# State outputs of a hybrid S5 decoder layer over 128 stacked rows, by an exchange of halves through DRAM, and the table products in one piece

## The chip, the cores and the metric

One core of a Trainium2 chip runs the whole kernel. The metric is device time in microseconds, the median of several runs. All times below are microseconds, unless ns is said.

## What is computed

One decoder layer is run for a prompt of 512 tokens and for 8 samples of 8 tokens each, together T = 576 tokens of width 1024: input projection, attention, a state-space branch (S5), merge, MLP, and an embedding gate. The change lies in the S5 branch, whose essence is

```
bu_re = einsum('btgc,gpc->btgp', ug, bb_re)        # 32 groups g of 16 channels c, 64 states p
bu_im = einsum('btgc,gpc->btgp', ug, bb_im)
_, _, hr, hi = associative_scan(combine, (ar, ai, bu_re, bu_im), axis=1)
y = einsum('btgp,gcp->btgc', hr, c_re) - einsum('btgp,gcp->btgc', hi, c_im)
y = y.reshape(bsz, t, D_SSM) + d_skip * uf
```

## The kernel before, in words

The tokens are cut into 72 chunks of CH = 8. Within a chunk the S5 output is a product with a 128x128 table per group (`Tm`: 8 steps times 16 channels on either side). Across chunks only the state at the chunk's border counts: `Hb` holds it, as real and imaginary part, for 16 pairs of groups. On the 128 partitions lie the 64 states of the even group of a pair (rows 0 to 63) and of the odd group (rows 64 to 127). `CA` holds, in the same layout, the powers that take a border state to the 8 outputs of its chunk. The output of group g in a PSUM bank is `Tm[g] . UT[g]` (128 rows) plus two products of 64 rows, `CA re . Hb re` and `CA im . Hb im`.

Three kinds of TensorE work stand between the dense products in this stretch:
- table blocks (event `vs`): products `bb . CA`, 16 columns wide over 64 rows, of which `Tm` is made. ScalarE copies them from PSUM to the tile `vs`; GpSimd adds the skip term (event `vd`), stores `vs` to DRAM and, once it has landed (semaphore `vs_spilled`), reads it back into `Tm` in eight loads, one per 16 partitions (event `tload`, semaphore `t_in`).
- the scan over the chunk borders (events `scan` 0 to 5), on VectorE in `Hb`: two products, one sum over both parts, and two sums of one part each per level. Its own semaphore is `scanned`.
- output blocks 0 to 3 (event `y`): 8 groups each, into two banks; ScalarE applies gelu, GpSimd stores.

A dense unit is one 128-wide slice of the input weights against all 576 tokens: 48 matmuls (8 slices of the contraction, three products of high and low halves, two column ranges). It waits at its start for the low half of its weights (`w_lo`), which VectorE makes three units ahead, after ScalarE has cast the high half, and for its PSUM bank, of which there are two in turn. The units in question are, in order, the gate units G2, G3, G4, G5, G6, G7 and the value units V0, V1, V2, V3. ScalarE evicts a gate unit into `gst`, which has two slots; GpSimd stores each from there to DRAM. So the eviction of G7 waits until the store of G5 has landed (`gate_out`).

The order of the work is one list, written out in `schedule_of`. Each engine runs through it and does its part of every event, so the place of an event in the list is its place in every engine's queue: `event` adds it, `unit()` puts a dense unit there, `begin(4)` the first half of one. GpSimd's queue also holds the DMAs that it issues, SP's the weight loads.

In the order before, TensorE has: G2, table block of 32 matmuls, G3, block of 64, G4, block of 32, G5, G6, G7, V0, output block 0, half of V1, output 1, rest of V1, output 2, half of V2, output 3, rest of V2, the final states, V3.

Of the kernel before, what the change touches and what calls it, by code (L numbers as in the profile page):

```python
# [25 lines left out]
ALU = mybir.AluOpType  # L26
# [5 lines left out]
P = 128  # L32
# [92 lines left out]
def schedule_of(units):  # L125
# [214 lines left out]
    event("sfinal", place=0)  # L340
    unit()
# [222 lines left out]
def build(nc, i, o):  # L564
# [4 lines left out]
    with ctx:  # L569
# [277 lines left out]
        u_d = nc.dram_tensor("u_spill", [AT, CH, P, NCH], F32, kind="Internal").ap()  # L847
        y_d = nc.dram_tensor("y_spill", [CH, GC, G, NCH], F32, kind="Internal").ap()
# [97 lines left out]
        def full_of(job):  # L946
            return psum_full[jobs[job][0]]
# [8 lines left out]
        def read(job):  # L956

            return free_of(job), jobs[job][1] + 1
# [127 lines left out]
        def _(pool):  # L1086
# [85 lines left out]
            for e in schedule:  # L1172
# [25 lines left out]
                elif k == "vd":  # L1198
# [4 lines left out]
                    for n in (6, 7):  # L1203
                        pool.wait_ge(*read(("vs", n)))
# [15 lines left out]
                elif k == "tload":  # L1220
# [3 lines left out]
                    for n in range(CH):  # L1224
                        pool.dma_start(Tm[GC * n:GC * n + GC, :, GC * n:P],
                                      vs_d[:, :, 0:P - GC * n]).then_inc(t_in, 16)
                elif k == "y" and a[1] == 1:
# [97 lines left out]
        def _(scalar):  # L1325
# [137 lines left out]
            for e in schedule:  # L1463
# [107 lines left out]
                elif k == "vs":  # L1571
                    scalar.wait_ge(*full(e))
                    if a[0] == 0:
# [143 lines left out]
        def _(vector):  # L1717
# [147 lines left out]
            for e in schedule:  # L1865
# [220 lines left out]
                elif k == "final":  # L2086
# [3 lines left out]
                    for q in range(2):  # L2090
                        c = sq8[:, q, 0, :].unsqueeze(1).unsqueeze(3).to_broadcast([P, 2, GP, 9])
                        tt(t9[q][:], src, c, ALU.mult).then_inc(count.up(dve_steps), 1)
                    vector.wait_ge(*count.last)
# [196 lines left out]
        def _(tensor):  # L2290
# [205 lines left out]
            for e in schedule:  # L2496
# [85 lines left out]
                elif k == "vs" and a[0] % 2 == 0:  # L2582

                    both = [("vs", a[0] + odd) for odd in range(2)]
# [4 lines left out]
                    for c in range(4):  # L2589
                        for part in range(2):  # L2590
                            for odd in range(2):
                                g = 4 * a[0] + odd + 2 * c
                                r = slice(64 * odd, 64 * odd + 64)
                                ins = mm(bank(both[odd])[0:GC, P * c:P * c + P], bb[r, part, g // 2, :],
                                         CA[r, part, g // 2, 0:CH, :].rearrange("q k c -> q (k c)"), part == 0, part == 1)
                                if c == 3 and part == 1:
                                    ins.then_inc(full_of(both[odd]), 1)
# [37 lines left out]
                elif k == "y" and a[1] == 0:  # L2635
# [9 lines left out]
                    for c in range(4):  # L2645
                        out = [bank(job)[:, NCH * c:NCH * c + NCH] for job in both]
                        for odd in range(2):
                            g = 8 * q + 2 * c + odd
                            mm(out[odd], Tm[:, g, :], UT[:, g, :], True)
                        for part in range(2):  # L2650
                            for odd in range(2):
                                r = slice(64 * odd, 64 * odd + 64)
                                ins = mm(out[odd], CA[r, part, 4 * q + c, 1:CH + 1, :].rearrange("q k c -> q (k c)"),
                                         Hb[r, part, 4 * q + c, :], False, part == 1)
                                if c == 3 and part == 1:
                                    ins.then_inc(full_of(both[odd]), 1)
# [202 lines left out]
```

## Time and profile before

| | |
|---|---|
| median of 3 runs | 928.38 (928.04 to 929.18) |
| span of the profiled execution (its whole time is not given apart) | 926.8 |
| TensorE busy | 912.9, 98% |
| VectorE busy | 603.9, 65% |
| ScalarE busy | 442.2, 48% |
| GpSimd busy | 91.5, 10% |

In the timeline each row is a run of like instructions: start, busy time, engine, source line, operation, output and inputs, and how many. An f32 product is shown as two matmuls. A pair of brackets gives the idle time before the row and what ended it. The view of the transfers gives rates in 40 equal slices of its window and, for each issue, the time to landing.

### The profile page before, as it was taken

How to read it: one execution, taken by the hardware profiler on the slowest of the kernel's cores; microseconds unless marked ns; L12 is line 12 of the kernel's file. 1: busy time of each engine (PE TensorE's matmuls, PEld its weight loads, DVE VectorE, ACT ScalarE, POOL GpSimd, SP SyncE). 2: the span in 40 equal slices, each digit the busy share in tenths (PEclk: the TensorE clock that was granted, in tenths of full speed). 3: DMA queues.
4: the chain of work that ended last, by engine and by line, in shares of the span. 5: the costliest groups of instructions: out<-in, count | busy, mean ns of one | idle time of the engine just before them, and what ended most of it. 6: DMA issues, size and time to landing. Idle time of an engine off the chain costs nothing.

```text
span 926.8 us, 17665 instructions
## 1 busy us (share of the span) xinstructions
PE 912.9 (98%) x7414; PEld 886.4 (96%) x7414; DVE 603.9 (65%) x815; ACT 442.2 (48%) x663; POOL 91.5 (10%) x143
## 2 busy tenths in 40 slices
PE   6999999999999999999999999999999999999998
PEld 5999999999999889999999999999999999999998
DVE  6689699511777746474568566666676666778453
ACT  7446323223776535444356544444444444446532
POOL 5390033202001210100000000000000000000000
PEclk9999999999999999999999999999999999999999
DMA  8531554824423585522223322222323222242202
GB/s 234 127 92 48 151 160 109 185 84 147 128 71 108 186 286 204 172 69 71 89 69 92 91 86 83 87 89 91 92 79 91 84 90 92 91 138 71 69 5 99
DMA packets 134694, 102.19 MB, mean 110 GB/s; under 512 B 18560, under 2 KB 124408, under 8 KB 134584
## 3 DMA queue, kind: packets, MB, share of 16 engines
q1 hardware_dynamic: 129096, 83.38, 30.5%
q0 software_dynamic: 5424, 17.65, 6.2%
q8 instruction: 59, 0.97, 0.4%
q14 instruction: 19, 0.16, 0.1%
q10 hardware_dynamic: 96, 0.04, 0.0%
HBM read 88.71 MB, written 12.21 MB: 109 GB/s over the span
## 4 chain that ended last, share of the span: by engine, by line
PE 92%; DVE 3%; ACT 2%; issue 1%; DMA 0%; SPq 0%; ACTq 0%; DVEq 0%
PE dense L2294 65%; PE banks L2294 20%; PE scoreA L2294 3%; PE banks L2481 2%; PE dense L2481 1%; PE scoreB L2294 1%; DVE Llo L1745 1%; ACT t L1626 1%; DVE t L2118 1%; ACT whi L1333 1%; DMA xtok<-in_x_prompt 0%; DVE Ssum L1721 0%; DVE sm L2176 0%; DVE wlo L1745 0%; ACT yh L1672 0%
## 5 line engine op out<-in xcount | busy, mean ns | idle before, releaser
L1745 DVE TENSOR_TENSOR wlo<-wraw,whi 128x1024 fp32r<-128x1024 f32 (+2 forms) x139 | 152.6, 1103 | 101.3 <-ACT whi L1333 89.0
L2294 PE MATMUL dense<-hid,whi 128*128 128x256 f32 (+1 forms) x1024 | 176.7, 294 | 0.1
L2294 PE MATMUL dense<-act_hi,whi 128*128 128x256 f32 (+1 forms) x736 | 167.4, 298 | 1.0 <-issue 0.7
L2294 PE MATMUL dense<-act_lo,whi 128*128 128x256 f32 (+1 forms) x736 | 163.3, 293 | 0.0
L2294 PE MATMUL dense<-act_hi,wlo 128*128 128x256 f32 (+1 forms) x736 | 163.3, 293 | 0.0
L2294 PEld LDWEIGHTS dense<-hid,whi 128*128 128x128 f32 x1024 | 152.5, 187 | 0.5 <-issue 0.3
L1333 ACT CAST whi<-wraw 128x1024 fp32r<-128x1024 f32 x100 | 109.9, 1101 | 45.6 <-PE banks L2294 44.1
L2294 PEld LDWEIGHTS dense<-act_hi,whi 128*128 128x128 f32 x736 | 123.4, 188 | 4.7 <-issue 3.3
L2294 PEld LDWEIGHTS dense<-act_lo,whi 128*128 128x128 f32 x736 | 124.1, 188 | 0.0
L2294 PEld LDWEIGHTS dense<-act_hi,wlo 128*128 128x128 f32 x736 | 124.0, 187 | 0.0
L2294 PE MATMUL dense<-hid,wlo 128*128 128x256 f32 (+1 forms) x512 | 108.8, 293 | 0.0
L2294 PEld LDWEIGHTS dense<-hid,wlo 128*128 128x128 f32 x512 | 85.4, 187 | 0.0
L2294 PE MATMUL banks<-XT,whi 128*128 128x288 f32 x416 | 83.7, 294 | 0.0
L1349 ACT CAST whi<-wsum 128x512 fp32r<-128x512 f32 x52 | 32.3, 621 | 86.3 <-PE dense L2294 63.6
L1826 DVE TENSOR_TENSOR R<-R,dense 128x576 f32<-128x576 f32 x64 | 48.0, 750 | 34.9 <-PE dense L2294 34.9
L2294 PEld LDWEIGHTS banks<-XT,whi 128*128 128x128 f32 x416 | 66.4, 188 | 0.0
L2294 PE MATMUL banks<-XT,wlo 128*128 128x288 f32 x208 | 61.3, 295 | 0.0
L2294 PE MATMUL dense<-yh,whi 128*128 128x256 f32 (+1 forms) x256 | 47.9, 300 | 0.5 <-ACT sg L1424 0.3
L1144 POOL DMA_DIRECT2D ptok<-in_p_prompt x4 | 2.2, 550 | 445.2 <-PE banks L2294 433.2
L2294 PE MATMUL banks<-act_hi,wlo 128*128 128x288 f32 x156 | 45.9, 294 | 0.0
L2294 PE MATMUL banks<-act_lo,whi 128*128 128x288 f32 x156 | 45.9, 294 | 0.0
L2294 PE MATMUL banks<-act_hi,whi 128*128 128x288 f32 x156 | 45.8, 294 | 0.0
(367 smaller groups left out, 1590.4 us busy)
## 6 DMA issues: line engine op xcount, KB each, us to landing
wraw<-in_w_in SPq DMA_DIRECT2D x32, 512.0 KB, 5.1
wraw<-in_w_up SPq DMA_DIRECT2D x32, 512.0 KB, 4.0
wraw<-in_w_down SPq DMA_DIRECT2D x32, 512.0 KB, 3.6
gates_spill<-gst POOLq DMA_DIRECT2D x16, 288.0 KB, 3.0
page<-in_cache_k SPq DMA_DIRECT2D x16, 256.0 KB, 7.9
page<-in_cache_v SPq DMA_DIRECT2D x16, 256.0 KB, 7.3
wraw<-in_w_out SPq DMA_DIRECT2D x8, 512.0 KB, 3.7
wraw<-in_w_ple_gate SPq DMA_DIRECT2D x8, 512.0 KB, 3.6
```

The lines of the kernel that those rows point to most:

```text
L1144: pool.dma_start(ptok[0:n, t % 2, :], src).then_inc(x2_in[t % 2], 16)
L1333: nc.scalar.copy(by_channel(u, whi[:, wslot(u), :]), by_group(u, wraw[:, u % NRAW, :])).then_inc(count.up(w_hi), 1)
L1349: nc.scalar.copy(wblock(whi, u, j), src).then_inc(count.up(w_hi), 1)
L1626: nc.scalar.activation(t1[h % 2][:], zflat(h), ACT.Exp, bias=bias[:, h:h + 1]).then_inc(count.up(z_free), 1)
L1745: return nc.vector.tensor_tensor(out=lo, in0=whole, in1=f32(hi), op=ALU.subtract)
L1826: nc.vector.tensor_tensor(out=R[:, m % 8, :], in0=R[:, m % 8, :], in1=prod(job), op=ALU.add).then_inc(count.upto(*read(job)), 1)
L2118: nc.vector.scalar_tensor_tensor(out=t2[h % 2][:], in0=zflat(h), scalar=bias[:, h:h + 1], in1=t1[h % 2][:], op0=ALU.add, op1=ALU.max).then ...
L2294: return nc.tensor.matmul(out, lhsT, rhs, start=start, stop=stop, skip_group_check=True)
L2481: return nc.tensor.transpose(out, in_, ident[0:rows, 0:rows])
```

## The change

1. The table products are one event pair in place of four, directly after G2. The four pairs of groups of a quarter go to four column groups (output partitions 0, 32, 64, 96), the two groups of a pair to two banks. ScalarE copies the result in eight copies of the same size as before.
2. After the Tm loads, GpSimd exchanges halves of `CA` through DRAM: the imaginary part of rows 0 to 63 and the real part of rows 64 to 127 go out, and each comes back in the other's place. Afterwards part 0 holds real and imaginary part of the even group in 128 rows, part 1 those of the odd group. The same is done with `Hb` behind the scan.
3. The output blocks use one product of 128 rows per group for the states. They stand one and a half dense units later: V0, V1, half of V2, output 0, rest of V2, output 1, half of V3, output 2, rest of V3, output 3.
4. The final states are formed right behind the last scan level; the exchange waits for them (`scanned` 7).

```diff
@@ schedule_of
     for lvl in range(6):
         event("scan", lvl)
+        if lvl == 5:
+            event("final")
         unit()
...
-        for i in ((), (0, 1), (2, 3, 4, 5), (6, 7), (), ())[lvl]:
-            event("vs", i, place=2 * (i // 2 % 2) + i % 2)
+        if lvl == 1:
+            for odd in range(2):
+                event("vs", odd, place=odd)
         if lvl == 3:
             event("vd")
             event("tload")
+            event("swap_out", "tables")
+            event("swap_in", "tables")
         if lvl in (3, 4):
             unit()
+    event("swap_out", "states")
+    event("swap_in", "states")
+    unit()
+    begin(4)
     for q in range(4):
         for side in range(2):
             event("y", q, side, place=2 * (q % 2) + side)
         if q % 2 == 0:
+            unit()
+        else:
             begin(4)
-        else:
-            unit()
-        if q == 0:
-            event("final")
...
     event("sfinal", place=0)
     unit()
-    unit()
@@ GpSimd
+                elif k in ("swap_out", "swap_in"):
...
+                    if k == "swap_out":
...
+                            pool.wait_ge(scanned, 7)
+                        pool.dma_start(memory[0], part_im[0:NS]).then_inc(vs_spilled, 16)
+                        pool.dma_start(memory[1], part_re[NS:P]).then_inc(vs_spilled, 16)
+                    else:
+                        pool.wait_ge(vs_spilled, 16 * (3 if a[0] == "tables" else 5))
+                        pool.dma_start(part_re[NS:P], memory[0]).then_inc(t_in, 16)
+                        pool.dma_start(part_im[0:NS], memory[1]).then_inc(t_in, 16)
@@ ScalarE
-                    g0 = 8 * (a[0] // 2)
-                    nc.scalar.copy(vs[:, g0 + a[0] % 2:g0 + 8:2, :],
-                                   bank(e)[0:GC, :].rearrange("p (a b) -> p a b", a=4)).then_inc(
-                                       count.upto(*read(e)), 1)
+                    for c in range(4):
+                        ins = nc.scalar.copy(vs[:, 2 * c + odd:G:8, :],
+                                             bank(e)[32 * c:32 * c + GC, :].rearrange("p (a b) -> p a b", a=4))
+                    ins.then_inc(count.upto(*read(e)), 1)
@@ TensorE, vs
-                    for c in range(4):
+                    for n in range(4):
                         for part in range(2):
-                            for odd in range(2):
-                                g = 4 * a[0] + odd + 2 * c
-                                r = slice(64 * odd, 64 * odd + 64)
-                                ins = mm(bank(both[odd])[0:GC, P * c:P * c + P], bb[r, part, g // 2, :],
-                                         CA[r, part, g // 2, 0:CH, :].rearrange("q k c -> q (k c)"), part == 0, part == 1)
...
+                            for c in range(4):
+                                for odd in range(2):
+                                    r = slice(64 * odd, 64 * odd + 64)
+                                    ins = mm(bank(both[odd])[32 * c:32 * c + GC, P * n:P * n + P], bb[r, part, 4 * n + c, :],
+                                             CA[r, part, 4 * n + c, 0:CH, :].rearrange("q k c -> q (k c)"),
+                                             part == 0, part == 1)
@@ TensorE, y
-                        tensor.wait_ge(t_in, 16 * CH)
-                        tensor.wait_ge(scanned, 6)
+                        tensor.wait_ge(t_in, 16 * (CH + 4))
...
                         for odd in range(2):
                             g = 8 * q + 2 * c + odd
-                            mm(out[odd], Tm[:, g, :], UT[:, g, :], True)
-                        for part in range(2):
-                            for odd in range(2):
-                                r = slice(64 * odd, 64 * odd + 64)
-                                ins = mm(out[odd], CA[r, part, 4 * q + c, 1:CH + 1, :].rearrange("q k c -> q (k c)"),
-                                         Hb[r, part, 4 * q + c, :], False, part == 1)
...
+                            mm(out, Tm[:, g, :], UT[:, g, :], True)
+                            ins = mm(out, CA[:, odd, 4 * q + c, 1:CH + 1, :].rearrange("q k c -> q (k c)"),
+                                     Hb[:, odd, 4 * q + c, :], False, True)
```

GpSimd's queue from the skip term on, before (`psum_free5` and `psum_free4` are the evictions of the dense bank that the gate to be stored was in):

```order
L1095 TENSOR_TENSOR dti<-ident,dd 16x512
L1095 TENSOR_TENSOR vs<-vs,dti 16x32x16 [waits psum_free3,psum_free2,pool_steps]
L1207 DMA vs_spill<-vs 16x4096 [waits vs_ready]
L1225 DMA Tm<-vs_spill 16x4096 [waits vs_spilled,tm_zero]
...
L1225 DMA Tm<-vs_spill 16x32x16
L1248 DMA gates_spill<-gst 128x576 [waits psum_free5]
L1248 DMA gates_spill<-gst 128x576 [waits psum_free4]
L1248 DMA gates_spill<-gst 128x576 [waits psum_free5]
L1231 DMA y_spill<-ygelu 128x576 [waits psum_free1,psum_free0]
```

and with the change, from the last Tm load on:

```order
L1233 DMA Tm<-vs_spill 16x32x16
L1247 DMA ca_spill<-CA 64x2304 [waits psum_full1,psum_full0]
L1248 DMA ca_spill<-CA 64x2304
L1251 DMA CA<-ca_spill 64x2304 [waits vs_spilled]
L1252 DMA CA<-ca_spill 64x2304
L1274 DMA gates_spill<-gst 128x576 [waits psum_free5]
L1274 DMA gates_spill<-gst 128x576 [waits psum_free4]
L1274 DMA gates_spill<-gst 128x576 [waits psum_free5]
L1247 DMA hb_spill<-Hb 64x1152 [waits scanned]
L1248 DMA hb_spill<-Hb 64x1152
L1251 DMA Hb<-hb_spill 64x1152 [waits vs_spilled]
L1252 DMA Hb<-hb_spill 64x1152
```

The four table transfers, with a wait between them, stand ahead of the gate stores of G5, G6 and G7, and the four of the states behind them.

TensorE at output block 0, before:

```order
L2294 MATMUL banks<-UT,Tm 128x72 [waits psum_free0,psum_free1,scanned,t_in]
L2294 MATMUL banks<-UT,Tm 128x72
L2294 MATMUL banks<-Hb,CA 128x72 x4
L2294 MATMUL banks<-UT,Tm 128x72 x2
L2294 MATMUL banks<-Hb,CA 128x72 x4
```

and with the change:

```order
L2322 MATMUL banks<-UT,Tm 128x72 [waits psum_free1,psum_free0,t_in]
L2322 MATMUL banks<-Hb,CA 128x72
L2322 MATMUL banks<-UT,Tm 128x72
L2322 MATMUL banks<-Hb,CA 128x72
L2322 MATMUL banks<-UT,Tm 128x72
```

The block has 16 f32 products instead of 24, and 72 more dense matmuls stand ahead of the first.

## Rows read from the trace of the kernel before

**Rows 1.** The page: busy times of the engines, share of the span, instructions

```profile
PE 912.9 (98%) x7414; PEld 886.4 (96%) x7414; DVE 603.9 (65%) x815; ACT 442.2 (48%) x663; POOL 91.5 (10%) x143
```

**Rows 2.** Timeline, TensorE: the table blocks, and the start of G6

```profile
130.67 0.43 PE L2294 MATMUL dense<-act_hi,wlo 128*128 128x256 f32 x2
131.03 1.92 PE L2294 MATMUL banks<-CA,bb 64*16 64x128 f32 x32
132.89 0.53 PE L2294 MATMUL dense<-act_hi,whi 128*128 128x256 f32 x2
...
139.41 3.67 PE L2294 MATMUL banks<-CA,bb 64*16 64x128 f32 x64
...
157.81 0.43 PE L2294 MATMUL dense<-act_hi,whi 128*128 128x256 f32 x2
158.07 0.42 PE L2294 MATMUL dense<-act_lo,whi 128*128 128x256 f32 x2
```

**Rows 3.** Timeline, TensorE: output block 0 and what follows it

```profile
176.77 0.56 PE L2294 MATMUL banks<-UT,Tm 128*128 128x72 f32 x4
177.26 0.67 PE L2294 MATMUL banks<-Hb,CA 64*128 64x72 f32 x8
...
181.44 0.53 PE L2294 MATMUL dense<-act_hi,whi 128*128 128x256 f32 x2
181.81 0.42 PE L2294 MATMUL dense<-act_lo,whi 128*128 128x256 f32 x2
```

**Rows 4.** Timeline, VectorE: scan level 3 and the low halves around it

```profile
145.39 1.22 DVE L1745 TENSOR_TENSOR wlo<-wraw,whi 128x1024 fp32r<-128x1024 f32 x1
146.64 3.89 DVE L1721 TENSOR_TENSOR sc<-Hb,sq 128x1760 f32<-128x1760 f32 x2
150.57 5.93 DVE L1721 TENSOR_TENSOR Hb<-Hb,sc 128x1760 f32<-128x1760 f32 x3
156.42 2.35 DVE L1745 TENSOR_TENSOR wlo<-wraw,whi 128x1024 fp32r<-128x1024 f32 x2
```

**Rows 5.** Timeline, GpSimd (POOL): from G4's gate store to G7's

```profile
150.58 0.54 POOL L1248 DMA_DIRECT2D gates_spill<-gst  x1 [9.57 <-ACT gst L1414]
155.85 0.56 POOL L1207 DMA_DIRECT2D vs_spill<-vs  x1 [0.29 <-POOL vs L1095]
160.62 4.91 POOL L1225 DMA_DIRECT2D Tm<-vs_spill  x8 [4.21 <-DMA vs_spill<-vs]
165.53 1.13 POOL L1248 DMA_DIRECT2D gates_spill<-gst  x2
175.37 0.54 POOL L1248 DMA_DIRECT2D gates_spill<-gst  x1 [8.71 <-ACT gst L1414]
```

**Rows 6.** Timeline, ScalarE: the eviction of G7

```profile
174.42 0.65 ACT L1414 ACTIVATE gst<-dense 128x576 f32<-128x576 f32 x1 [8.50 <-DMA gates_spill<-gst]
```

**Rows 7.** Timeline, TensorE: 20 transposes; 16 matmuls on four column groups

```profile
122.51 2.35 PE L2481 MATMUL banks<-ident,qk 128*128 128x128 f32 x20
...
341.61 0.65 PE L2294 MATMUL scoreA<-KTb,Qb 128*32 128x128 f32 x16
```

**Rows 8.** Transfers issued from 140 to 210: KB each, median us to landing

```profile
wraw<-in_w_in SPq DMA_DIRECT2D x8, 512.0 KB, 4.2
y_spill<-ygelu POOLq DMA_DIRECT2D x4, 288.0 KB, 2.4
vs_spill<-vs POOLq DMA_DIRECT2D x1, 256.0 KB, 4.2
...
Tm<-vs_spill POOLq DMA_DIRECT2D x1, 32.0 KB, 8.1
```

**Rows 9.** Transfers, 380 to 388: 40 slices, the last eight x_sample's (64 partitions)

```profile
GB/s 164 184 246 225 348 389 348 471 348 430 471 369 430 410 369 348 451 394 435 438 300 382 438 415 404 369 379 394 422 430 351 179 166 184 159 156 146 236 156 207
```

**Rows 10.** Timeline, TensorE: the first transposes of 128x128

```profile
8.54 3.67 PE L2481 MATMUL dense<-ident,xtok 128*128 128x128 f32 x16 [0.60 <-DVE xtok L1874]
12.05 2.20 PE L2481 MATMUL banks<-ident,xtok 128*128 128x128 f32 x15
```

More of the change, by code:

```diff
@@ L1202, in _ @@
                     pool.wait_ge(*count.last)
-                    for n in (6, 7):
-                        pool.wait_ge(*read(("vs", n)))
+                    for odd in range(2):
+                        pool.wait_ge(*read(("vs", odd)))
                     tt(vs[:, :, 0:GC], vs[:, :, 0:GC], dti[:], ALU.add).then_inc(count.up(vs_ready), 1)
@@ L1226, in _ @@
                                       vs_d[:, :, 0:P - GC * n]).then_inc(t_in, 16)
+                elif k in ("swap_out", "swap_in"):
+                    part_re, part_im, memory = (
+                        (CA[:, 0].rearrange("p g k c -> p (g k c)"), CA[:, 1].rearrange("p g k c -> p (g k c)"), ca_d)
+                        if a[0] == "tables" else
+                        (Hb[:, 0].rearrange("p g n -> p (g n)"), Hb[:, 1].rearrange("p g n -> p (g n)"), hb_d))
+                    if k == "swap_out":
+                        if a[0] == "tables":
+                            for odd in range(2):
+                                pool.wait_ge(*full(("vs", odd)))
+                        else:
+                            pool.wait_ge(scanned, 7)
+                        pool.dma_start(memory[0], part_im[0:NS]).then_inc(vs_spilled, 16)
+                        pool.dma_start(memory[1], part_re[NS:P]).then_inc(vs_spilled, 16)
+                    else:
+                        pool.wait_ge(vs_spilled, 16 * (3 if a[0] == "tables" else 5))
+                        pool.dma_start(part_re[NS:P], memory[0]).then_inc(t_in, 16)
+                        pool.dma_start(part_im[0:NS], memory[1]).then_inc(t_in, 16)
                 elif k == "y" and a[1] == 1:
@@ L2091, in _ @@
                         c = sq8[:, q, 0, :].unsqueeze(1).unsqueeze(3).to_broadcast([P, 2, GP, 9])
-                        tt(t9[q][:], src, c, ALU.mult).then_inc(count.up(dve_steps), 1)
-                    vector.wait_ge(*count.last)
+                        tt(t9[q][:], src, c, ALU.mult).then_inc(count.up(dve_steps if q == 0 else scanned), 1)
+                    vector.wait_ge(dve_steps, count.made[dve_steps])
+                    vector.wait_ge(scanned, 7)
                     tt(Fh[:], Fh[:], t9[0][:], ALU.add).then_inc(count.up(dve_steps), 1)
@@ L2581, in _ @@
                     ins.then_inc(full_of(e), 1)
-                elif k == "vs" and a[0] % 2 == 0:
-                    both = [("vs", a[0] + odd) for odd in range(2)]
+                elif k == "vs" and a[0] == 0:
+                    both = [("vs", odd) for odd in range(2)]
                     tensor.wait_ge(ca_ready, 1)
@@ L2588, in _ @@
                             tensor.wait_ge(*free(job))
-                    for c in range(4):
+                    for n in range(4):
                         for part in range(2):
-                            for odd in range(2):
-                                g = 4 * a[0] + odd + 2 * c
-                                r = slice(64 * odd, 64 * odd + 64)
-                                ins = mm(bank(both[odd])[0:GC, P * c:P * c + P], bb[r, part, g // 2, :],
-                                         CA[r, part, g // 2, 0:CH, :].rearrange("q k c -> q (k c)"), part == 0, part == 1)
-                                if c == 3 and part == 1:
-                                    ins.then_inc(full_of(both[odd]), 1)
+                            for c in range(4):
+                                for odd in range(2):
+                                    r = slice(64 * odd, 64 * odd + 64)
+                                    ins = mm(bank(both[odd])[32 * c:32 * c + GC, P * n:P * n + P], bb[r, part, 4 * n + c, :],
+                                             CA[r, part, 4 * n + c, 0:CH, :].rearrange("q k c -> q (k c)"),
+                                             part == 0, part == 1)
+                                    if n == 3 and part == 1 and c == 3:
+                                        ins.then_inc(full_of(both[odd]), 1)
                 elif k in ("kout", "vout"):
@@ L2645, in _ @@
                     for c in range(4):
-                        out = [bank(job)[:, NCH * c:NCH * c + NCH] for job in both]
                         for odd in range(2):
                             g = 8 * q + 2 * c + odd
-                            mm(out[odd], Tm[:, g, :], UT[:, g, :], True)
-                        for part in range(2):
-                            for odd in range(2):
-                                r = slice(64 * odd, 64 * odd + 64)
-                                ins = mm(out[odd], CA[r, part, 4 * q + c, 1:CH + 1, :].rearrange("q k c -> q (k c)"),
-                                         Hb[r, part, 4 * q + c, :], False, part == 1)
-                                if c == 3 and part == 1:
-                                    ins.then_inc(full_of(both[odd]), 1)
+                            out = bank(both[odd])[:, NCH * c:NCH * c + NCH]
+                            mm(out, Tm[:, g, :], UT[:, g, :], True)
+                            ins = mm(out, CA[:, odd, 4 * q + c, 1:CH + 1, :].rearrange("q k c -> q (k c)"),
+                                     Hb[:, odd, 4 * q + c, :], False, True)
+                            if c == 3:
+                                ins.then_inc(full_of(both[odd]), 1)
                 elif k == "zz":
```

5 lines of the change are left out of this document (4 added, 1 removed).

## The prediction

> **What bounds the kernel now.** I read the page first, then TensorE in order of time around the two places that the change touches, then VectorE, ScalarE and GpSimd over the same stretch, and last the transfers. TensorE is busy 98% of the span [rows 1]: what counts is work on TensorE, or time for which it is made to wait. In this stretch it is never idle: a dense unit of 48 matmuls is 24 pairs that start 0.26 us apart (157.81 to 158.07 [rows 2]), 6.33 us in all.
>
> The table blocks stand between G2 and G5 with 32, 64 and again 32 matmuls [rows 2] (an f32 product is two matmuls in the trace). The first holds up the dense stream from 130.67 + 0.26 = 130.93 to 132.89, and the first dense pair after it takes 0.37 instead of 0.26 (181.44 to 181.81 [rows 3]): 2.06 us. The second, by its 3.67 instead of 1.92 us, costs 3.8, the third 2.06 again: together 7.9. The four output blocks cost 4.67 + 0.11 = 4.78 us each: in one, four runs of 4 table matmuls and four of 8 state matmuls alternate, (181.44 - 177.26) / 7 = 0.60 us a run behind the first [rows 3], although the 8 state matmuls run two by two (upper and lower 64 rows at once) and fill only four places.
>
> VectorE is the hidden second bound. From 145 to 169 its instructions follow one another with no idle time [rows 4]: scan level 3, then the low halves of G6's and G7's weights, the first ready at 156.42 + 1.21 = 157.63. G6 starts at 157.81 [rows 2]. So G6 has 0.2 us to spare, no more.
>
> GpSimd's queue is the third. It stores G4's gate at 150.58, the vs table at 155.85, waits 4.2 us for it, issues the eight Tm loads from 160.62, and only then stores G5's and G6's gates (165.53) [rows 5]. ScalarE therefore evicts G7 only at 174.42, after 8.50 us of waiting for G5's store [rows 6]. That costs nothing today because V1, which reuses G7's PSUM bank, starts after output block 0, at 181.44 [rows 3].
>
> **The change on TensorE.** Output blocks: 32 matmuls of full 128 rows, no switch between 64 and 128 rows. 20 transposes with weights of the same 128x128 take 2.35 us, the last one's tail of 0.27 included [rows 7], 0.11 each. At 0.112 a place a block takes 32 x 0.112 = 3.6 us against 4.78. Saved: 4 x 1.2 = 4.9 us. The number of places is unchanged; only the switches go.
>
> Table block: 128 matmuls, now 8 at once (four groups of 16 columns times two halves of rows). Four at once, on four column groups, are in the trace: 16 matmuls in 0.65 us, the last one's tail of 0.27 included [rows 7], so 0.1 for four. With 8 at once: 16 places x 0.11 + 0.3 = 2.1 us, saved 5.8; bounds 2.1 and 7.3 (only the halves overlap, as now).
>
> **Where the table saving goes.** The first block keeps its length, so G3 still ends at 139.3. G4 then follows at once and ends at 145.6, 3.8 us earlier. G5 waits for its low half (145.39 + 1.22 = 146.6) and ends at 152.95. G6 waits for 157.63, for the scans are where they were: TensorE idles 4.7 us. Of 5.8 us, 0.1 is left at G6's start. What is late next is VectorE. G7 ends at 170.4, V0 at 176.7, as before.
>
> ScalarE's eight copies (as many as before and of the same size, two after each old small block) now stand in one run of some 4 us from 133.0, ahead of a cast whose low half VectorE takes up at 145.39 [rows 4]: no cost, as long as those 7 us of slack stand.
>
> **Where the exchanges go.** They are GpSimd's, in its queue ahead of G5's gate store, and the second half of each waits for the first to land. All 3.8 us earlier than before: G4's store 146.8, first Tm load 156.8. Before, the last Tm load landed at 164.9 + 8.1 = 173.0 [rows 5, 8], 12.4 us after the first issue; now 169.2. Then:
> - tables out: two transfers of 576 KB from 64 partitions. The one plain 64-partition transfer, the x_sample load, moves 146 to 184 GB/s where the 128-partition ones before it move 350 to 450 [rows 9]. 590 kB / 0.19 = 3.1 us each, 6.2: landed 175.4.
> - GpSimd resumes 0.55 us after a landing (155.85 + 4.2, next issue 160.62 [rows 5, 8]). A single y_spill of 288 KB lands in 2.4 us [rows 8], 0.8 of it data at 380 GB/s, so 1.6 us is fixed. Tables in: 176.0 + 1.6 + 6.2 = 183.8.
> - G5's store lands 0.8 us later, 184.6; half a microsecond for weight loads between: **ScalarE evicts G7 at about 185.0** (174.42 before).
>
> V1 now comes straight after V0 and needs that bank: TensorE can go at 176.7 and is let go at 185.7. Stall 9.0 us.
>
> Unknown is whether two transfers on opposite halves overlap. If they did fully, both would move at 380 and each leg would take 3.1. The eight Tm loads go to eight different groups of 16 partitions, and 1152 KB of them need 12.4 us; the one vs store from 16 partitions moves 256 KB in 4.2 [rows 8]. They did not overlap, so I take them one after the other. The Trainium skill, in "SBUF — State Buffer", section "Can I just issue two DMAs to hit both halves?", speaks against this exchange: two transfers at partitions 0 and 64 gave 6% more than one. By that page, as an estimate, the eviction comes at 184.3.
>
> State exchange: issued behind G7's store, which starts 0.95 us after the eviction (175.37 against 174.42 [rows 5, 6]). Out: 1.6 + 0.8 (G7's data) + 2 x 1.55 = landed 6.4 after the eviction; back: 0.55 + 1.6 + 3.1: 11.7 after it. TensorE gets to block 0 at 0.7 + 9.5 (V1 and half of V2) = 10.2 after it, so it would wait 1.5 us. But after 9 us of standing still I expect the clock to have fallen from 2.4 to 1.2 GHz: in the old trace the granted clock reads 1.00 (2.4 GHz) in every slice, yet the first 16 transposes after the idle start take 3.67 us, and the next 15 take 2.20 with two of them still slow [rows 10]. Some 20 matmuls at 0.1 more each: 1.8 us, which makes it 12.0 and covers the state exchange. Block 0 starts at 197.0 either way within 0.3.
>
> The Trainium skill ("DMA: Bandwidth & Descriptors", "Anatomy of one DMA — SWDGE (gpsimd) path") has a fixed 2.0 us for such a transfer where rows 8 give 1.6. By it, as an estimate, three legs take 0.4 us more each and the sum is about 1 us higher.
>
> **Sum.** Before, block 0 starts at 176.77 with 72 dense matmuls (9.5 us) fewer behind it: comparable 186.3. Now 197.0: +10.7. Output blocks -4.9. Everything after is the same work and follows TensorE. +5.8 us on a span of 926.8. The profiled execution's span is 1.6 us under the median; on the median of 928.4 that is **934.2 us**. About 0.2% (1.9 us) is what a measurement can tell from no change.
>
> **Rivals.**
> - A, the halves overlap or run at full rate (13%). Two legs of 3.1 us less: eviction at 178.8, stall 2.8 us, no fall of the clock, block 0 at 189.0: 2.7 - 4.9 = -2.2, 926.2 us. For it: 128-partition transfers reach 380 GB/s. Against it: [rows 8, 9]. This is the side of faster, and it decides at an eviction near 181.1: the exchanges have to be 4 us shorter than my sum.
> - B, weight loads of SP take the engines between (10%). Eight loads of 512 KB lie in 70 us of the old trace, each 1.4 us of all engines at 380 GB/s [rows 8], and they come in pairs after the paired casts. If a pair lies in front of the tables and one load in front of the states: +3 and +1.5, 938.7 us. For it: the load of 512 KB lands in 4.2 us at the median, so it is itself held up by what lies in front.
> - C, the 8 groups don't run at once (8%). Block of 7.3 us: G4 ends 1.5 later than before instead of 3.8 earlier, and the whole GpSimd chain with it: +5.2, 939.4 us. Four at once only: +1.7.
> - D, the saving arrives whole (4%): neither the gate stores nor the scans hold TensorE, 928.4 - 4.9 - 5.8 = 917.7. Against it stands VectorE without a gap [rows 4]. If only the gate store doesn't hold it: 928.4 - 5.0 = 923.4.
>
> **Numbers.** My forecast has 65%: 929 to 937 on its own, by 4 us less in the table legs or 3 more. Below 0.2% slower lie A, D and a tenth of the forecast's own share. Faster 0.13 (most of A, and D), same 0.11 (rest of A, short end of the forecast), slower 0.76. Range 926.5 to 939.0: both ends of the transfer rate but one in five left out (D, the worst of B and C).
>
> **What would show it.** Right: one table block of about 2 us at 131.0; TensorE idle before G6 by 4 to 5 us, released by VectorE; the four table transfers on GpSimd between 161.7 and 177, a gap of 10 us or more between out and in; ScalarE's G7 eviction at 183 to 187 and TensorE idle from 176.7 until just after; output blocks of 3.6 us without a switch. Wrong: an eviction before 181; a table block over 4 us; G6 starting well before 157.6; output blocks still near 4.7.

## The result, and the profile after

The changed kernel takes **937.66** in the median of six executions (936.89 to 943.19), against 928.67 for the kernel before, measured beside it: a ratio of 1.0114, 95% interval 1.0099 to 1.0128, so between 9 and 12 us slower. Four executions lie between 936.9 and 937.7, two at 942.2 and 943.2. The forecast had 934.2. The profiled execution took 937.27, with a span of 935.5, 8.7 over that of before [rows 1]. Its first table block starts 0.41 later than that of before, so 0.41 has to be taken off times from here on when they are set beside the old ones.

From its page, busy times and the granted clock in 40 slices:

```profile
PE 906.8 (97%) x7350; PEld 882.5 (94%) x7350; DVE 604.4 (65%) x815; ACT 443.1 (47%) x663; POOL 96.3 (10%) x151
...
PEclk9999998989999999999999999999999999999999
```

TensorE is busy for 6.1 us less, though the span is longer: it is made to wait. The two slices that read 8 (140 to 164 and 187 to 210) hold the stretches at a low clock behind the two long waits. The timeline of TensorE, with the table block, the two long waits and the start of output block 0:

```profile
131.44 2.00 PE L2322 MATMUL banks<-CA,bb 64*16 64x128 f32 x128
...
158.12 0.85 PE L2322 MATMUL dense<-act_hi,whi 128*128 128x256 f32 x2 [4.53 <-DVE wlo L1772]
...
188.44 0.82 PE L2322 MATMUL dense<-act_hi,whi 128*128 128x256 f32 x2 [9.14 <-ACT gst L1440]
...
200.88 0.44 PE L2322 MATMUL banks<-UT,Tm 128*128 128x72 f32 x2 [0.58 <-DMA Hb<-hb_spill]
201.16 0.39 PE L2322 MATMUL banks<-Hb,CA 128*128 128x72 f32 x2
201.38 0.39 PE L2322 MATMUL banks<-UT,Tm 128*128 128x72 f32 x2
```

The block of 128 matmuls, 2.00 us long, stands in place of three that were busy for 1.92, 3.67 and 1.92 [rows 2]. G6 still starts where it did, behind 4.53 us of idling until VectorE has its low half. V1 starts at 188.44, after 9.14 us for ScalarE's eviction of G7. Output block 0 starts at 200.88 instead of 176.77 [rows 3] with 9.5 us of dense work moved ahead of it, so 14.6 late (14.2 with the 0.41 taken off). Inside the block a pair of matmuls starts every 0.22 us, without the pattern of fours and eights.

ScalarE's eviction of G7 and, on GpSimd, the transfers ahead of it:

```profile
187.64 0.65 ACT L1440 ACTIVATE gst<-dense 128x576 f32<-128x576 f32 x1 [19.37 <-DMA gates_spill<-gst]
```

```profile
157.93 4.91 POOL L1233 DMA_DIRECT2D Tm<-vs_spill  x8 [4.09 <-DMA vs_spill<-vs]
162.84 0.58 POOL L1247 DMA_DIRECT2D ca_spill<-CA  x1
...
178.00 0.53 POOL L1251 DMA_DIRECT2D CA<-ca_spill  x1 [14.06 <-DMA ca_spill<-CA]
...
179.03 1.13 POOL L1274 DMA_DIRECT2D gates_spill<-gst  x2
```

The stores of G5's and G6's gates are issued at 179.03 (165.53 before [rows 5]), because GpSimd stands for 14.06 us between the two halves of the table exchange. ScalarE stands behind that for 19.37 us, where it was 8.50 before [rows 6]. The transfers issued between 140 and 215, KB each and median us to landing:

```profile
wraw<-in_w_in SPq DMA_DIRECT2D x9, 512.0 KB, 6.4
...
ca_spill<-CA POOLq DMA_DIRECT2D x2, 576.0 KB, 13.8
CA<-ca_spill POOLq DMA_DIRECT2D x2, 576.0 KB, 7.8
...
Tm<-vs_spill POOLq DMA_DIRECT2D x1, 32.0 KB, 12.0
```

The last Tm load takes 12.0 us to land instead of 8.1 [rows 8], so all are in at 162.3 + 12.0 = 174.3, 16.4 after the first issue instead of 12.4. The weight loads of SP take 6.4 instead of 4.2. The two kinds share the engines, which the windows show (us, TensorE busy, granted clock, DMA share, GB/s):

```profile
160.00:164.00 4.00, 4.00 (x24) 0.70 1.06 174
164.00:172.00 8.00, 8.00 (x63) 1.00 1.12 137
172.00:177.00 5.00, 5.00 (x40) 1.00 1.03 334
177.00:180.00 3.00, 2.29 (x18) 1.00 1.22 293
180.00:186.00 6.00, 0.00 (x0) 0.74 0.99 240
```

By the DMA share all 16 engines are busy from 160 to 186, at very different rates; the rates are those of all queues together. And the same view around the two long waits:

```profile
153.00:158.00 5.00, 0.59 (x5) 0.76 0.46 52
156.00:158.00 2.00, 0.00 (x0) 0.50 0.00 0
158.00:162.00 4.00, 3.88 (x16) 0.50 0.80 102
162.00:166.00 4.00, 4.00 (x31) 0.95 1.18 191
...
183.00:188.00 5.00, 0.00 (x0) 0.50 0.66 190
188.00:192.00 4.00, 3.56 (x15) 0.50 0.61 146
192.00:194.00 2.00, 2.00 (x13) 0.71 0.82 235
194.00:200.00 6.00, 6.00 (x48) 1.00 0.92 247
```

Behind both waits TensorE works at a granted clock of 0.50 (1.2 GHz): 16 and 15 matmuls in 3.9 and 3.6 us of work, where a window of 4 us at full clock holds up to 33. The clock has fallen before the waits end: at 155.6, 2.0 us into the first, and at 182.9, 3.6 us into the second. It is back at 162.4 and at 193.1. So it is low for 6.8 and for 10.2 us, and TensorE has work in 4.3 and 4.7 us of that. The forecast had this behind the second wait only.

### The profile page after: what moved, and what is told of

It reads as the page before. It is cut to its first block, busy times and chain, and to the rows that moved or that the text cites. A ratio compares the mean times of both kernels' runs of the same rounds, so it can differ in the third digit from the quotient of the medians.

```text
span 935.5 us, 17543 instructions
## 1 busy us (share of the span) xinstructions
PE 906.8 (97%) x7350; PEld 882.5 (94%) x7350; DVE 604.4 (65%) x815; ACT 443.1 (47%) x663; POOL 96.3 (10%) x151
## 4 chain that ended last, share of the span: by engine, by line
PE 86%; DMA 5%; DVE 3%; ACT 3%; POOL 1%; issue 1%; SPq 0%; ACTq 0%; DVEq 0%; POOLq 0%
PE dense L2322 60%; PE banks L2322 19%; PE scoreA L2322 3%; PE banks L2509 2%; DMA ca_spill<-CA 2%; DMA gates_spill<-gst 1%; PE scoreB L2322 1%; DMA xtok<-in_x_prompt 1%; DVE Llo L1772 1%; DMA Hb<-hb_spill 1%; ACT t L1653 1%; DVE t L2146 1%; ACT whi L1359 1%; DMA hb_spill<-Hb 1%; POOL Tm L1233 0%
## 5 line engine op out<-in xcount | busy, mean ns | idle before, releaser
L2322 PEld LDWEIGHTS dense<-act_hi,whi 128*128 128x128 f32 x736 | 125.1, 190 | 18.9 <-issue 12.1
```

The costliest lines, as they stand in the source:

```text
L2322: return nc.tensor.matmul(out, lhsT, rhs, start=start, stop=stop, skip_group_check=True)
```

## Experiments

All times are medians; the kernel before, beside them, had 928.2 to 928.6. Granted clocks and waits are those of the one profiled execution of each.

**Where the table exchange stands.** In this kernel it comes directly behind the table products; the numbers of `vs_spilled` that are waited for change with it.

```diff
         if lvl == 1:
             for odd in range(2):
                 event("vs", odd, place=odd)
+            event("swap_out", "tables")
+            event("swap_in", "tables")
         if lvl == 3:
             event("vd")
             event("tload")
-            event("swap_out", "tables")
-            event("swap_in", "tables")
```

> The changed kernel, with the exchange of the tables issued by GpSimd directly behind the table products (before G3's gate store) instead of behind the eight Tm loads; its counts of landed transfers are renumbered to suit, nothing else. Theory (the stall comes from the place of the table exchange in GpSimd's queue): the tables are out and back by 150, G5's store lands near 174, ScalarE evicts G7 at 174 to 175, V1 starts by 177.5, the state exchange (some 12 us) lies wholly beside V1 and half of V2 or ends 1 to 2 us behind them, output block 0 starts near 187 to 189; 923.5 to 926 us. Rival (SP's weight loads that share the DMA engines, not the place in the queue, make the delay): Tm's last load still lands 16 us after the first is issued, G7's eviction comes at 177 to 178, V1 waits 1 to 2 us and the state exchange 3 more: 928 to 930 us.

Measured: 924.94 (five executions, four of them 924.8 to 925.2, one 932.2, its mean clock 0.993 where the others have 0.996 to 0.998), span 923.2. Because of the one, the ratio's interval holds 1: 0.9951 to 1.0015. GpSimd and ScalarE in its timeline:

```profile
133.70 0.55 POOL L1247 DMA_DIRECT2D ca_spill<-CA  x1 [0.99 <-PE banks L2322]
...
141.78 0.51 POOL L1251 DMA_DIRECT2D CA<-ca_spill  x1 [6.99 <-DMA ca_spill<-CA]
...
162.47 0.58 POOL L1274 DMA_DIRECT2D gates_spill<-gst  x1
```

```profile
173.79 0.65 ACT L1440 ACTIVATE gst<-dense 128x576 f32<-128x576 f32 x1 [5.50 <-DMA gates_spill<-gst]
```

The exchange is the same, the weight loads too; it now lies beside G3 and G4. G7 is evicted at 173.79 instead of 187.64, V1 has no wait, and block 0 starts at 188.62 without one. The medians differ by 12.7 us, and 12.1 of it is in the trace of the change: 9.14 of waiting ahead of V1, 2.4 of low clock behind it, 0.58 at block 0. The rival of the expectation, the weight loads, is not enough by itself to hold V1: the last Tm load still takes 11.3 us to land here, and nobody waits for it.

**No exchange at all**, and **no exchange with the old output products**. The first leaves out the eight transfers, so that its output blocks multiply unexchanged halves, and what TensorE waits for ahead of block 0 changes with it; the second puts back the old products as well.

```diff
-            event("swap_out", "tables")
-            event("swap_in", "tables")
...
-    event("swap_out", "states")
-    event("swap_in", "states")
```

> The changed kernel without both exchanges (eight transfers left out); the output blocks keep their new products of 128 rows, so the S5 outputs are computed from unexchanged halves. Theory: no stall ahead of V1, no fall of the clock there; the new order costs nothing by itself, the table products give nothing, and the four output blocks save 4.9 us together: 923.5 us (923 to 924.5). Rival (the later place of the output blocks or the longer waiting of the scan chain costs by itself): 926 us or more.

> The changed kernel without both exchanges and with the old output products (one of 128 rows, two of 64 rows per group), in the new order. Theory (the switches between products of 128 and of 64 rows cost 1.2 us per output block): 4.9 us above the run without the exchanges, so level with the kernel before, 928.4 us (within 0.7). Rival (most of the gain of the new blocks is in places, or hidden): less than 2.5 us above the run without the exchanges.

Measured: 924.80 (ratio 0.9964, 0.9950 to 0.9978) and 930.42 (1.0020, 1.0010 to 1.0030). Without the exchange the kernel is no faster than with the early one: moved, the exchange is hidden wholly. The starts of output blocks 0 and 1 in the two timelines, new products first:

```profile
188.82 0.34 PE L2318 MATMUL banks<-UT,Tm 128*128 128x72 f32 x2
...
195.56 0.34 PE L2318 MATMUL banks<-UT,Tm 128*128 128x72 f32 x2
```

```profile
189.26 0.56 PE L2318 MATMUL banks<-UT,Tm 128*128 128x72 f32 x4
...
197.19 0.56 PE L2318 MATMUL banks<-UT,Tm 128*128 128x72 f32 x4
```

6.74 against 7.93 from one block to the next, with the same dense work between: 1.19 a block, 4.8 in all, as the prediction worked out (1.2 and 4.9). The medians differ by more, 5.6; the other 0.8 was not traced. And the two kernels are 1.3 and 2.0 us slower than was expected. Both traces have a wait of 4.4 to 4.5 us ahead of G6 and a granted clock of 0.50 behind it; the next kernel shows what that costs.

**The table products alone**, in the kernel before.

```diff
-        for i in ((), (0, 1), (2, 3, 4, 5), (6, 7), (), ())[lvl]:
-            event("vs", i, place=2 * (i // 2 % 2) + i % 2)
+        if lvl == 1:
+            for odd in range(2):
+                event("vs", odd, place=odd)
```

> The kernel before with only the table products changed: one event pair of 128 matmuls behind G2, eight copies. Theory (VectorE's scan 3 and the low half of G6's weights hold G6 at 157.8, so the 5.8 us saved are given back as a wait ahead of G6): TensorE idle 4 to 5 us before G6, time within 0.5 us of the kernel before; if the clock falls after that wait, up to 2 us slower. Rival (the saving arrives whole): 922.6 us.

Measured: 930.51 (1.0024, 1.0015 to 1.0034): **2.1 us slower**, although 5.8 us of work are gone. The windows around G6:

```profile
153.00:158.00 5.00, 0.57 (x5) 0.99 0.46 52
158.00:162.00 4.00, 4.00 (x19) 0.58 0.84 108
162.00:166.00 4.00, 4.00 (x33) 1.00 1.18 195
```

TensorE waits 4.43 us for VectorE and then runs 19 matmuls in 4 us. Granted 0.58 of full speed for 4 us, it loses 1.7 us, and nothing behind it takes that up. The other executions lose as much or more: six of the ten have a mean clock of 0.995 or 0.996, the profiled one 0.998. So the saving doesn't merely vanish in the wait: the clock falls behind the wait, and the kernel gets slower.

**The same with that wait removed**: VectorE makes the low half of G6's weights ahead of scan level 3.

```diff
-        event("scan", lvl)
+        if lvl != 3:
+            event("scan", lvl)
         unit()
+        if lvl == 3:
+            event("scan", lvl)
```

> The kernel before with the new table products alone and scan level 3 behind its dense unit. The new products alone were 2.1 us slower than the kernel before, with TensorE idle for 4.4 us ahead of G6 and the granted clock at 0.50 behind it. Theory: with that wait gone the clock stays at 1.00 and part of the 5.8 us saved arrives: V0 starts 3 us earlier, output block 0 then waits for the scans (final level at 174.4) or for Tm (173 to 174.5), 926 us (925 to 927.5), that is 3.5 to 5 us under the run of the products alone. Rival: the clock falls all the same, 928.4 us or more.

Measured: 924.68 (0.9958, 0.9941 to 0.9974), 5.8 under the products alone. The clock stays at 1.00, and one wait of 1.29 is left, ahead of V0:

```profile
153.00:158.00 5.00, 5.00 (x40) 1.00 0.61 80
158.00:162.00 4.00, 4.00 (x33) 1.00 0.90 119
```

That is more than the 3.5 to 5 expected.

**The same step in the kernel with the early exchange.**

> The kernel with the tables exchanged early, and scan level 3 put behind the dense unit whose event it stood ahead of, so that VectorE makes the low half of G6's weights before it. Theory (the wait of 4.5 us ahead of G6 costs itself and 2.1 us more, since the granted clock is 0.50 for some 3.5 us behind it): no wait ahead of G6, granted clock 1.00 throughout, at most 2 us of wait ahead of V0 instead, block 0 at 186 to 187 because the state exchange (10.4 us from the last scan at 176) now holds it: 2 to 2.5 us under the run with the tables exchanged early, 922.5 us (921.5 to 923.5). Rival (the granted clock falls for another reason, such as the table products themselves): the slow stretch stays, 924.5 us or more.

Measured: 928.88 (1.0010, 1.0000 to 1.0019), so **4 us slower** than without the step; the expectation (922.5) missed. Start of output block 0, and windows:

```profile
187.53 0.44 PE L2325 MATMUL banks<-UT,Tm 128*128 128x72 f32 x2 [3.98 <-DMA Hb<-hb_spill]
```

```profile
183.00:187.00 4.00, 0.55 (x5) 1.00 0.92 220
188.00:198.00 10.00, 10.00 (x47) 0.50 0.08 30
198.00:204.00 6.00, 6.00 (x51) 0.98 0.00 0
```

Up to block 0 it went nearly as expected: no wait ahead of G6, block 0 at 187.5 (186 to 187 expected), 1.1 earlier than without the step, the state exchange now in the way. What was not expected is behind it: after 3.98 us of idling at a granted clock of 1.00 the clock is 0.50 for 10.2 us (188.0 to 198.2), all of it with work on TensorE, and 5.1 us go. The forecast's idea that a wait costs its length, and some 2 us if it is a long one, was too simple. The clock was low just as long around the 9.14 us wait of the changed kernel, but 5.5 of those 10.2 us lay in the wait itself. What sets the length of the low stretch, 3.4 to 10.2 us in these traces, was not tested.

**Weight loads held back**, to take them away from the Tm loads and the tables in the changed kernel:

```diff
+                if u == FIRST["v"] + 3:
+                    sync.wait_ge(t_in, 16 * CH)
+                elif u == FIRST["v"] + 4:
+                    sync.wait_ge(t_in, 16 * (CH + 2))
                 weights(u)
```

> The changed kernel; SP holds back the weight loads of V3 and of the three units behind it: the first two until the eight Tm loads have landed, the next until the tables are back. Theory (the weight loads share the DMA engines with the Tm loads at 160 to 168 and with the tables' way back at 177 to 180, and that is why ScalarE's eviction of G7 came 2.2 us later than forecast): the last Tm load lands 12.5 to 13 us after the first issue instead of 16.4, the tables out follow at once, G7's eviction comes 3 to 5 us earlier, at 183 to 184.5; 933 to 935 us. Rival (the Tm loads are slow in themselves, and the engines have room for both): landing and eviction within 1 us of the changed kernel's, 937 us; if the weights then come too late for their casts, slower still.

Measured: 940.31 (1.0133, 1.0116 to 1.0150). GpSimd and ScalarE:

```profile
157.58 4.90 POOL L1237 DMA_DIRECT2D Tm<-vs_spill  x8 [4.11 <-DMA vs_spill<-vs]
...
172.40 0.53 POOL L1255 DMA_DIRECT2D CA<-ca_spill  x1 [8.82 <-DMA ca_spill<-CA]
```

```profile
182.99 0.65 ACT L1444 ACTIVATE gst<-dense 128x576 f32<-128x576 f32 x1 [15.05 <-DMA gates_spill<-gst]
```

The mechanism held: the wait between the two halves is 8.8 instead of 14.1, the last Tm load lands 8.0 after its issue instead of 12.0, and G7 is evicted at 182.99 instead of 187.64 (4.3 earlier, since the times of this trace run 0.35 ahead of those of the change). The time did not (933 to 935 expected): the delayed loads fall on the state exchange, and the wait moves to output block 0 (3.16 us), with the same price as above:

```profile
195.00:199.00 4.00, 1.05 (x8) 1.00 0.93 211
199.00:209.00 10.00, 9.79 (x46) 0.53 0.12 41
```

**Output blocks half a unit later in the changed kernel**, for the two executions at 942 to 943.

> The changed kernel with the output blocks half a dense unit later, nothing else. In the changed kernel's profiled execution block 0 waited 0.6 us for the state exchange and the clock held, yet two of its six executions took 5 us longer. Theory (in those two the wait at block 0 was longer and the clock fell behind it, as in the run with a wait of 4.0 us there): with some 3 us of slack ahead of block 0 no execution is 5 us longer, all lie within 1.5 us of 937.0. Rival (they come from elsewhere): one execution in three is again 4 to 6 us above the others.

Measured: 937.88 (four executions, 936.98 to 938.45; 1.0101, 1.0086 to 1.0115). In line with the theory (no wait at block 0 in its trace, but one of 0.91 us ahead of the transposes of V); but if two executions in six are long ones, four in a row without one come by chance one time in five. The two long executions of the changed kernel were not profiled. Their mean granted clock was 0.987, that of the other four 0.990 to 0.993, so more time at the low clock is on record; that a wait at block 0 brought it is likely, not shown.

**Towards the best order.** The kernel with the early exchange and scan 3 behind its unit, its output blocks one unit later; then with the products of the final states (`sfinal`) ahead of output block 3 as well; then that with the blocks only half a unit later:

```diff
     unit()
-    begin(4)
+    unit()
     for q in range(4):
+        if q == 3:
+            event("sfinal", place=0)
         for side in range(2):
             event("y", q, side, place=2 * (q % 2) + side)
         if q % 2 == 0:
-            unit()
-        else:
             begin(4)
+        else:
+            unit()
...
-    event("sfinal", place=0)
-    unit()
```

> The kernel with the tables exchanged early and scan level 3 behind its unit, and now the output blocks one dense unit later (V0, V1, V2, half of V3, output 0, ...). The same without this step took 928.9 us with output block 0 ready at 187.5 after 4.0 us of waiting for the state exchange and the granted clock at 0.50 for the 10 us behind it. Theory (the wait costs its 4.0 us and 5 us of clock): TensorE reaches block 0 near 190, without waiting, the clock stays at 1.00 all the way: 919.5 us (918.5 to 921). Rival (the output blocks are slow for another reason, or their later place costs elsewhere, such as the later gelu and the y stores): 924 us or more.

> As the run with the output blocks one dense unit later (923.5 us; 921.7 to 927.5, TensorE waited 0.8 us for the copy of the final states and 0.95 for those of the values, directly behind the last output block), with the final states' products moved ahead of output block 3. Theory (those 1.8 us and some of the spread come from the final states standing between the last block and the values): both waits go, 921.5 us (920.5 to 922.5), spread under 2 us. Rival (the values' copies on ScalarE are behind the last gelu in any case): one wait of 1 to 2 us stays, 923 us or more.

> Tables exchanged early, scan level 3 behind its unit, output blocks half a unit later, and the final states' products ahead of output block 3. The state exchange ended at 187.5 in the run without the last two steps, TensorE reaches block 0 at 186.7: a wait of 0.8 us or less. Theory (it is the length of the wait that decides on the clock: 0.8 to 1.3 us left it at 1.00 elsewhere, 3.2 and 4.0 us did not): no fall of the clock in most executions, 920.5 us (919.5 to 922), perhaps single ones 5 us longer. Rival: any wait ahead of the output blocks brings the clock down, 926 us or more.

Measured, in this order: 923.46 (0.9956, 0.9939 to 0.9972; seven executions from 921.65 to 927.49), 923.88 (0.9952, 0.9939 to 0.9965) and **920.85** (0.9926, 0.9913 to 0.9940). One unit later, the wait at block 0 and the fall of the clock are gone, but the time is 4 us above the 919.5 expected: now the transposes of V behind the last block wait (0.8 us for the copy of the final states, 0.95 for that of the values; the other 2 were not traced, and the mean clock of the slower executions, down to 0.996, has a part in the spread). With `sfinal` ahead of block 3 they wait 2.38 us for the copy of the values alone, and ScalarE, which makes it, waits for the y store:

```profile
217.37 2.51 ACT L1598 COPY vtok<-banks 128x512 f32<-128x512 f32 x5 [3.04 <-DMA y_spill<-ygelu]
```

So that expectation missed, and its rival held. With half a unit between block 3 and the values that wait is gone too. Block 0 is reached 0.17 us before the states arrive (timeline), and the clock holds (window):

```profile
187.18 0.44 PE L2325 MATMUL banks<-UT,Tm 128*128 128x72 f32 x2 [0.17 <-DMA Hb<-hb_spill]
```

```profile
180.00:190.00 10.00, 9.83 (x79) 1.00 0.76 199
```

920.85 beats the kernel before by 7.8 us and the change by 16.8; five of its six executions lie between 920.7 and 921.2, one is at 924.8, with a mean granted clock of 0.996 where the others have 0.999 or 1.00. There is no slack at block 0: TensorE already waits 0.17 us there.

## Why the prediction was right and wrong

The direction and the chain were right: slower, by a table exchange that stands ahead of the gate stores in GpSimd's queue and so holds ScalarE's eviction of G7 and with it V1. The size was not: +5.8 forecast, +8.7 in the profiled execution, +9 in the median, and more in the mean. The step that failed is the transfer sum up to the eviction of G7, in its term for weight loads (0.5 us there, 4.3 by the run with the loads held back); second to it, the clock behind the wait of G6 and the price of the one behind V1's. By the steps of the prediction:

- *Output blocks, -4.9.* Right: -4.8, from the distance of the blocks.
- *Table block, 2.1 us, and its saving gone.* Right as to the block (2.00) and the wait (4.53 against 4.7). **Wrong that this is all**: the clock falls behind it. In the change its 2.1 us are covered, since V1 waits for GpSimd and not for TensorE. With the products alone they were the whole result. The step weighed a fall of the clock for the 9 us wait and left it out for the 4.7 us wait, with nothing in the trace to part the two.
- *"Half a microsecond for weight loads between".* **This term was mis-sized**, and it is the larger miss: the eviction came 2.2 us later (187.64 - 0.41 against 185.0). The last Tm load landed 4.7 later than forecast (174.3 - 0.4 against 169.2): 4.0 by the longer loads, 0.7 because GpSimd's work on the skip term took that much longer (147.83 to 152.99 against 151.13 to 155.56), so that they began 3.1 us earlier than before and not 3.8. Holding the weight loads back removed 4.3 us. The eviction then came at 182.9 in the old trace's time, 1.6 ahead of the forecast without its half microsecond: the loads cost 4.3 instead of 0.5, and the transfers themselves were forecast 1.6 too long, which hid part of the miss. The prediction had the mechanism as rival B with one part in ten. It should have been in the sum: the first Tm load is issued together with two weight loads (157.93 and, in SP's queue, 158.10) which in the old trace were issued ahead of it (from 157.66 on, against 160.62), and the tables meet the next ones (167.35 and 169.56, some 13 us to landing). The Trainium skill ("DMA: Bandwidth & Descriptors", "Queues, rings and completion order") says that each engine serves the queues with work in turn, packet by packet. The traces agree as far as they can show it: loads of both queues take half as long again here, and the Tm loads go back to 8.0 us with the other queue held back.
- *The two halves one after the other at 190 GB/s, behind the Tm loads.* Too slow for the way out. By the view of the transfers, the bytes (MB) of GpSimd's queue (q0) and SP's (q1), in the change from 174.3, where the last Tm load has landed, to 177.5, and in the kernel with the early exchange from 135.5 to 139:

```profile
q1 hardware_dynamic: 1101, 0.55, 58.4%
q0 software_dynamic: 91, 0.60, 45.5%
...
q0 software_dynamic: 111, 0.84, 105.1%
q1 hardware_dynamic: 5, 0.00, 0.2%
```

Only 0.60 of the tables' 1.18 MB moved behind the last Tm load. The rest had gone beside the Tm loads: from 163.4 to 174.3 GpSimd's queue moved 1.48 MB, more than all eight Tm loads together (1.18). So the tables were out 3.1 us behind it and not 6.2. The rate of GpSimd's queue was 188 GB/s beside 172 of SP's, and 240 with hardly anything of SP's. The 334 of the window 172 to 177 are both queues and the end of the Tm loads. On the way back (180 to 186) all queues together moved 240, G5's and G6's stores among it, and the leg took 9.6 us up to the eviction instead of 9.0. The 190 were read from slices [rows 9] in which SP's queue has a part (0.17 of the 0.39 MB from 386 to 388), and two of the eight slices read 236 and 207. The Trainium skill ("SBUF — State Buffer", section "Can I just issue two DMAs to hit both halves?") gives 6% for the second half; as an estimate from that page's figure on the 190, the pair would move 201. The 240 are above that, but the 190 themselves come from mixed slices, and no run here has one half alone, so the 6% can be neither confirmed nor refuted.
- *A stall of 9.0 ahead of V1.* 9.14, and that is luck: the eviction came 2.2 later than forecast, and TensorE got there 2.2 later too (178.9 in the old trace's time against 176.7), held up by the low clock behind G6's wait.
- *From V1 to block 0, 11.3.* 12.4: the clock cost 2.4 (0.50 for the 4.7 us up to 193.1) instead of 1.8, and block 0 waited 0.58 for the states, which were said to be covered within 0.3.
- *Everything after follows TensorE.* Not quite: TensorE is 9.9 us late at 234.8 and 9.15 late at 387.1, and the span ends 8.7 late. Shortly ahead of 387 the old trace has 0.35 us of idling on TensorE that this one lacks; what took up the rest was not traced.

So block 0 starts at 200.47 in the old trace's time instead of 197.0: 2.3 from the transfers (with the restart behind the eviction), 1.1 from clock and wait. That is the miss in the profiled execution. Two executions in six lie 5 us above the rest. The amount is that of a low clock behind a wait at block 0, as in two kernels here, but those executions were not traced. The range stopped at 939.0 since no case had it.

## What to carry to other kernels

Where transfers move ahead of others in one queue, ask first whether they can stand where nobody waits behind them: the same exchange cost 12.7 us behind the Tm loads and nothing behind the products that last read the tables. A wait put onto TensorE has two prices, its length and what the low clock takes from the work behind it, 1.7 to 5.1 us in these traces; a saving that only turns into a wait of 4 us can make the kernel slower. And when a chain of transfers is moved by a few microseconds, look at which loads of other queues it now meets, and put them into the sum, not into a rival.

## What the runs showed of the hardware that was not expected

- Around waits of 4.4 to 9.1 us ahead of a dense unit the granted clock fell to 0.50, and the length of the wait did not say what it cost: 1.7 us behind the 4.43 us wait of the products alone (low from 157.9 to 161.4, all behind the wait), 2.1 behind the 4.53 us wait of the change (155.6 to 162.4), 2.8 behind the 4.83 us wait ahead of V1 with the loads held back (182.5 to 189.4), 2.4 behind the wait of 9.14 us (182.9 to 193.1). Lost is half of the part in which TensorE had work.
- Waits of 3.2 and 4.0 us ahead of an output block (32 matmuls 72 wide) were followed by 10.2 us at 0.50, without idle time on TensorE: 5 us lost, more than the wait itself. What came behind these waits differs from the cases above, and so does where in the low stretch the wait ended; the runs don't part the two.
- Waits of 0.6 to 2.4 us left the clock at 1.00 in the profiled executions (2.38 with `sfinal` ahead of block 3 and the blocks one unit later).
- With two transfers of 576 KB on opposite halves of the partitions under way, GpSimd's queue moved 240 GB/s where SP's moved almost nothing (135.5 to 139 with the early exchange), and 188 beside SP's 172 (174.3 to 177.5 in the change).
- 128 f32 matmuls of 64 rows and 16 columns took 2.00 us when they were spread over four column groups and both halves of the rows, where 32 of them on the two halves alone had taken 1.92 (131.44 in the change, 131.03 before).
